# Gated projection of the state space layer: high parts written block by block, low parts consumed one by one, and the combined outputs turned at other places

## The chip, the cores and the metric

The kernel runs on one core of a Trainium2 chip. The metric is the device time of one execution in microseconds (us); a kernel's time is the median of its runs.

## What is computed

One inference step of a hybrid decoder with two layers, for a prompt of 1024 tokens and 8 x 8 sample tokens with the same weights. All 1088 tokens stand side by side as columns (with 4 columns of padding: `T` = 1092). The first layer has three dilated attention groups and a state space layer (S5) side by side; the change lies in the tail of that layer:

```python
out_a = (num / den[..., None]).reshape(n, t, D_A)          # three attention groups combined
y, h_last = s5_scan(u, ...)                                # (tokens, 512)
zb = jax.nn.gelu(y)
out_b = zb * jax.nn.sigmoid(zb @ w_glu + b_glu)            # the gated projection, 512 x 512
mix = jnp.concatenate([out_a, out_b], axis=-1) @ w_out_ab  # 1024 x 1024
```

The products are taken in float32 as three products of split operands: a value is a high part (rounded to `fp32r`) plus a low part (the rest), and high x high, high x low and low x high are summed in PSUM.

## The kernel before, in words

**How a product is tiled.** Weights come in slots of 1.1 MB. SP loads a slot into `w_raw` (`feed`, line 351), POOL splits it into `w_hi` and `w_lo` (lines 656 and 658), and TensorE (PE) uses it in `features` (line 770). Two split buffers alternate, so POOL splits slot n + 2 when PE has finished slot n (`slot_done`). One output unit of 128 features is three PSUM banks of 364 columns. For each of its k-chunks of 128 input features PE runs 9 matmuls, line 784: three operand pairs times three column blocks. The units alternate between PSUM banks 0 to 2 and 3 to 5; banks 6 and 7 are left for turning tiles. The gated projection (slot `W_GLU`) has 4 units of 4 k-chunks, so 36 matmuls per unit; a slot of the output projection (`W_OUT`) has 2 units of 8 k-chunks.

**The stage around the change, per engine.** Every engine has its own program in order, tied by semaphores.

- PE computes the scan's block outputs in two halves (`block_outputs`, lines 1060 and 1065) for z = 0 and z = 1, two blocks r each, and turns them back to feature rows (line 1095). Then it waits until all four low parts of `zb` are made (`lo_made`, line 1099), and runs `features` on `W_GLU`. After each unit m `mixed_pair(m)` (line 1103) turns two of the eight tiles of `out_a` in banks 6 and 7 (line 1112), the first time after the load of `mix_in`, and from the second pair on after DVE has read both banks (`mix_low`). Before `W_OUT` it waits for all low parts and for `mix_low` 8.
- ACT copies the block outputs (line 1458), applies Gelu to each of four blocks r of `zb` (line 1467) and, after all four, writes the four high parts `z_hi` (`high`, line 1261, from the loop at 1470). In the GLU loop it takes each unit with Sigmoid (`take`, line 1271), copies the two turned tiles into the high part `h_hi` of the output projection's input (line 1485), and makes the high part of a gated unit one unit later.
- DVE clears the padding of `zb` (line 2142), makes the four low parts `z_lo` (`low`, line 1670), then per unit multiplies the sigmoid with `zb` (line 2152), makes the low part of the gated unit (line 1670), and makes the two low parts of the turned tiles (line 2158).
- SP loads `mix_in` when the last block output is made (`y_mm` 4). When everything of the layer's combined output is made (`LO_MIXED_A` and `mix_low` 8) it loads the old residual `xd` (4.4 MB) and goes on feeding slots, the next being slot 23. Slots 21 and 22 (the first two of `W_OUT`) have been loaded by then, and slot 21 is split.
- POOL splits slot 22 when PE has finished `W_GLU`.

`z_hi`, then `z_lo` lie in the region `xa`, which held `d_mat` (front part) and `b_mat` (back part) of the scan until shortly before.

Of the kernel before, what the change touches and what calls it, by code (L numbers as in the profile page):

```python
# [20 lines left out]
P = 128  # L21
# [87 lines left out]
def build(nc, a):  # L109
# [16 lines left out]
    with ExitStack() as ctx:  # L126
# [14 lines left out]
        def sem(name):  # L141
# [32 lines left out]
            [("ca", 2 * ST * 9 * 16, F32), ("ub", L_BLK * 512, F32)],  # L174
            [("kc_sb", 2 * T, F32), ("vc_sb", 9 * 256, F32), ("qc_st", 2048, F32), ("on_c", 1024, F32)])
        hid_hi, hid_lo = (hid_hi0, hid_hi1), (hid_lo0, hid_lo1)
        (xa, z_hi, z_lo, sp_t, qb, qs, so, c_acc, bt, _, x12, _, bm_e, d_mat, _, b_mat,
         cs_s, cs_t, ocs, cstat) = region(
            "xa", KC * T,
            [("z_hi", 4 * T, F32R), ("z_lo", 4 * T, F32R)],  # L180
            [("sp_t", 12 * P, F32), ("qb", 768, F32), ("qs", 12 * SAMPLE, F32), ("so", 256, F32), ("c_acc", 1024, F32)],
            [("bt", 4096, F32), ("e3", 32, F32), ("x12", 2 * 2304, F32)],
            [("e4", 4128, F32), ("bm_e", 4096, F32)],
# [52 lines left out]
        def tiles(t, n):  # L236

            return t[:, :].rearrange("p (n c) -> p n c", n=n)
# [441 lines left out]
        def _(pe):  # L680
# [86 lines left out]
                            mean_square(2, True)  # L767
                rms.add(6)

            def features(slot, XH, XL, kcs=KC, n_units=2, done=1, arriving=False, after={}, kcs_used=False):  # L770

                WH, WL = halves(slot, kcs)
                for m in range(n_units):
                    cols = slice(m * P, m * P + P)
                    s = m % 2
                    late(free[s], u.free[s].at)
                    u.free[s].add()
                    for kc in range(kcs):
                        if arriving and m == 0:
                            pe.wait_ge(lo_made, lo.add())  # L780
                        for w, x in ((WH, XH), (WL, XH), (WH, XL)):
                            first, last = kc == 0 and w is WH and x is XH, kc == kcs - 1 and x is XL
                            for c in range(3):
                                mm = pe.matmul(UNIT[s][:, c, :], w[:, kc, cols], x[:, kc, c * CH:(c + 1) * CH],  # L784
                                               start=first, stop=last)
                        if kcs_used and m == n_units - 1 and kc < kcs - 1:
                            mm.then_inc(kc_used, 1)
                    if m == n_units - 1:
                        mm.then_inc(slot_done, done)
                        u.done.add(done)  # L790
                    else:
                        mm.then_inc(full, 1)
                        u.full.add()
                    if m in after:
                        after[m]()
# [300 lines left out]
                    mm.then_inc(turn_mm, 1)  # L1096


            pe.wait_ge(lo_made, lo.add(4))
            slot_ready()  # L1100


# [9 lines left out]
                        mm = pe.transpose(psum[:, 6 + b, c * P:c * P + P], mix_in[:, t * 512 + c * P:t * 512 + c * P + P], ident[:, :])  # L1112
                    mm.then_inc(turned, 1)

            features(W_GLU, ZH, ZL, kcs=4, n_units=4, after={k: lambda k=k: mixed_pair(k) for k in range(4)})
            lo.add(4)


            lo.add()
# [1 line left out]
            for layer in range(2):  # L1121
# [50 lines left out]
                pe.wait_ge(lo_made, lo.at)  # L1172
                for k in range(3):
                    slot_ready()
                    features(W_OUT[layer] + k, HH, HL)
                mixed_tail(W_OUT[layer] + 3)

                up = W_FF[layer]
# [44 lines left out]
        def _(act):  # L1223
# [230 lines left out]
            for z in range(2):  # L1454
                for r in (2 * z, 2 * z + 1):
                    act.wait_ge(y_mm, r + 1)
                    for h in range(2):
                        act.activation(groups(YT, r, h), psum[:, 2 * r + h, :].rearrange("p (k s c) -> p k s c", k=4, s=L_BLK),
                                       ACT.Copy).then_inc(y_taken, 1)
                if z == 0:  # L1460
                    act.wait_ge(turn_mm, 1)
                    act.activation(ZB[:, :, 0:SAMPLE], psum[:, 4, 0:4 * SAMPLE].rearrange("p (m t) -> p m t", m=4),
                                   ACT.Gelu_apprx_tanh).then_inc(act_own, 1)
                    own.add()
                for r in (2 * z, 2 * z + 1):
# [10 lines left out]
            lo.add()  # L1476
            for m in range(4):
                if m >= 2:
                    act.wait_ge(lo_made, lo.at + m - 1)
                take(TMP[:, m % 2, :], m, m == 3, ACT.Sigmoid, bias=param[:, C_GLU + m:C_GLU + m + 1])  # L1480
                if m:
                    high(HH[:, 3 + m, :], TMP[:, (m - 1) % 2, :], scaled, scl.add())
                for b in range(2):
                    act.wait_ge(turned, n_turn.add())
                    act.activation(HH[:, 0:4, SAMPLE + (2 * m + b) * P:SAMPLE + (2 * m + b + 1) * P],
                                   psum[:, 6 + b, :].rearrange("p (k c) -> p k c", c=P), ACT.Copy).then_inc(mix_high, 1)
            high(HH[:, 7, :], TMP[:, 1, :], scaled, scl.add())
            lo.add(4)


            for layer in range(2):
                if layer == 1:
# [12 lines left out]
                    act.wait_ge(zeroed, 4)  # L1505
                    attend(0, H_C)
                    lo.add(8)
                    for n in range(NB):
# [139 lines left out]
        def _(dve):  # L1648
# [489 lines left out]
            dve.tensor_tensor(STS[:, 0], HV[:, 0, :, N_BLK + 1:], SX[0], ALU.add)  # L2138
            dve.tensor_tensor(STS[:, 1], HV[:, 1, :, N_BLK + 1:], SX[2], ALU.add)
            dve.tensor_copy(st_o[:, 0:2 * ST].rearrange("p (c j) -> p c j", c=2), HV[:, :, :, N_BLK]).then_inc(state_out, 1)  # L2140
            dve.wait_ge(turn_mm, 1)
            dve.memset(ZB[:, :, PADS:T], 0.0).then_inc(zeroed, 1)
            for m in range(4):
                low(ZL[:, m, :], ZB[:, m, :], ZH[:, m, :])


            dve.memset(HH[:, 0:4, PADS:T].bitcast(F32), 0.0)
            dve.memset(HL[:, 0:4, PADS:T].bitcast(F32), 0.0)
            low(HL[:, 0:4, 0:SAMPLE], tiles(oas, 4), HH[:, 0:4, 0:SAMPLE])
            for m in range(4):  # L2150
                dve.wait_ge(free[m % 2], UNITS_AT[W_GLU] // 2 + m // 2 + 1)
                dve.tensor_tensor(TMP[:, m % 2, :], TMP[:, m % 2, :], ZB[:, m, :], ALU.mult).then_inc(scaled, 1)
                low(HL[:, 4 + m, :], TMP[:, m % 2, :], HH[:, 4 + m, :])
                for b in range(2):
                    t = 2 * m + b
                    cols = slice(SAMPLE + t * P, SAMPLE + t * P + P)
                    dve.wait_ge(mix_high, t + 1)
                    dve.tensor_tensor(HL[:, 0:4, cols], psum[:, 6 + b, :].rearrange("p (k c) -> p k c", c=P), HH[:, 0:4, cols].bitcast(F32),
                                      ALU.subtract).then_inc(mix_low, 1)
            u.skip(4)  # L2160


# [302 lines left out]
```

## Time and profile before

| what | value |
|---|---|
| runs | 3629.39, 3631.47 and 3649.05 us; median 3631.47 us |
| the profiled execution | 3641.45 us, of which the profile's span is 3639.6 us |
| busy share of the span | PE 91%, weight loads 87%, DVE 39%, ACT 25%, POOL 21% |
| granted TensorE clock, mean | 0.955 of full speed |

The span is what the profile shows from the first instruction to the last. The busy share of PE is an average over stages; the stage of the change lies from about 1020 to 1135 us. In the page's 40 slices of 91 us it is the one from 1001 to 1092 us (busy tenths of PE 8, granted clock 7 tenths) and the one behind it.

Three views are read below. The chain of waits follows the work that ended last back to what released it. The waits give, for each engine, the idle time and what ended it. The windows give busy time and granted clock of each engine in a stretch: a clock of 0.50 is 1.2 GHz and 1.00 is 2.4 GHz.

### The profile page before, as it was taken

To read this page: it belongs to the slowest core of one execution; us is meant where nothing else is said; L and a number is where in the kernel's file an instruction comes from. 1 tells how busy PE (TensorE), PEld (TensorE's weight loads), DVE (VectorE), ACT (ScalarE), POOL (GpSimd) and SP (SyncE) were. 2 spreads that over 40 slices of the span, in tenths; PEclk is the share of its full clock that TensorE was granted. 3 is DMA by queue.
4 is the path that set the end of the run, shared out by engine and by line. 5 is a ranking of instruction groups with operands and counts; after the bars stand their busy time and mean duration, and the time that the engine had idled before them with its cause. 6 is when DMAs were issued, how large, how long until landed. Compare 5 with 4: busy or idle time off the path is not lost.

```text
span 3639.6 us, 50510 instructions
## 1 busy us (share of the span) xinstructions
PE 3310.4 (91%) x21025; PEld 3163.5 (87%) x21025; DVE 1402.4 (39%) x1852; ACT 907.6 (25%) x1876; POOL 779.6 (21%) x226
## 2 busy tenths in 40 slices
PE   5998999984578899999999899886989999999988
PEld 4997988983468799999999799876879999999988
DVE  7615012033442633333334571364254333333364
ACT  3116044061131500000001521474151000000151
POOL 2220220210002222333223222200112332233321
PEclk9999999987789999999999999998899999999999
DMA  3311320348802222221225021100112112222411
GB/s 112 120 66 39 116 89 26 114 156 292 282 28 87 87 84 95 84 83 63 92 95 203 25 94 43 42 0 32 74 74 78 55 64 80 80 80 80 161 38 62
DMA packets 84290, 325.26 MB, mean 89 GB/s; under 512 B 19056, under 2 KB 32176, under 8 KB 66096
## 3 DMA queue, kind: packets, MB, share of 16 engines
q1 hardware_dynamic: 84160, 323.41, 25.2%
q8 instruction: 96, 1.57, 0.2%
q14 instruction: 34, 0.28, 0.0%
HBM read 274.21 MB, written 107.46 MB: 105 GB/s over the span
## 4 chain that ended last, share of the span: by engine, by line
PE 79%; DVE 9%; ACT 6%; issue 3%; DMA 2%; SPq 1%; ACTq 0%; DVEq 0%
PE psum L784 61%; PE psum L809 6%; PE psum L856 2%; PE psum L725 2%; PE psum L881 2%; ACT pr L1313 1%; PE psum L759 1%; DVE stat L1810 1%; ACT pt L1321 1%; DVE xa L1733 1%; DVE sm L1805 1%; DVE rs L1680 1%; DVE h_lo L1670 1%; DVE xa L1741 1%; PE psum L983 1%
## 5 line engine op out<-in xcount | busy, mean ns | idle before, releaser
L656 POOL CAST w_hi<-w_raw 128x2184 fp32r<-128x2184 f32 x109 | 222.8, 2044 | 2782.3 <-PE psum L784 2096.4
L784 PE MATMUL psum<-h_hi,w_hi 128*128 128x364 f32 x2832 | 627.6, 330 | 16.6 <-DVE tmp L2232 6.8
L784 PE MATMUL psum<-h_lo,w_hi 128*128 128x364 f32 x2544 | 563.6, 329 | 5.9 <-DVE h_hi L1710 5.9
L658 POOL TENSOR_TENSOR w_lo<-w_raw,w_hi 128x2184 fp32r<-128x2184 f32 x109 | 542.7, 4979 | 8.7
L784 PEld LDWEIGHTS psum<-h_hi,w_hi 128*128 128x128 f32 x2832 | 494.9, 189 | 18.0 <-DVE tmp L2232 7.4
L784 PE MATMUL psum<-h_hi,w_lo 128*128 128x364 f32 x2304 | 509.6, 329 | 0.0
L2248 DVE TENSOR_TENSOR xa<-xa,psum 128x1092 f32<-128x1092 f32 x256 | 330.8, 1292 | 382.6 <-PE psum L784 382.3
L784 PEld LDWEIGHTS psum<-h_lo,w_hi 128*128 128x128 f32 x2544 | 441.7, 189 | 6.4 <-DVE h_hi L1710 6.2
L784 PEld LDWEIGHTS psum<-h_hi,w_lo 128*128 128x128 f32 x2304 | 400.6, 189 | 0.0
L1592 ACT ACTIVATE tmp<-tmp 128x1092 f32<-128x1092 f32 x64 | 71.6, 1118 | 1255.6 <-DVE tmp L2232 1255.6
L784 PE MATMUL psum<-hid_hi,w_hi 128*128 128x364 f32 x1536 | 338.7, 328 | 5.2 <-DVE xa L2248 5.2
L784 PE MATMUL psum<-hid_lo,w_hi 128*128 128x364 f32 x1536 | 339.9, 330 | 0.0
L784 PE MATMUL psum<-hid_hi,w_lo 128*128 128x364 f32 x1536 | 339.2, 329 | 0.0
L1805 DVE TENSOR_TENSOR sm<-psum,mask 128x512 f32<-128x512 f32 (+1 forms) x160 | 94.5, 590 | 515.0 <-PE psum L856 511.1
L2232 DVE SCALAR_TENSOR_TENSOR tmp<-psum,sq 128x1092 f32<-128x1092 f32 x64 | 82.7, 1295 | 533.4 <-PE psum L784 508.8
L784 PEld LDWEIGHTS psum<-hid_hi,w_hi 128*128 128x128 f32 x1536 | 267.8, 189 | 5.8 <-DVE xa L2248 5.8
L784 PEld LDWEIGHTS psum<-hid_lo,w_hi 128*128 128x128 f32 x1536 | 267.1, 188 | 0.0
L784 PEld LDWEIGHTS psum<-hid_hi,w_lo 128*128 128x128 f32 x1536 | 266.7, 188 | 0.0
L809 PE MATMUL psum<-w_hi,h_hi 128*128 128x256 f32 x648 | 184.9, 285 | 21.8 <-DVE h_lo L1670 20.1
L809 PE MATMUL psum<-w_hi,h_lo 128*128 128x256 f32 x648 | 183.8, 284 | 0.0
L1313 ACT ACTIVATE pr<-sm,stat 128x256 f32<-128x256 f32 (+1 forms) x320 | 147.1, 460 | 90.4 <-DVE stat L1810 45.3
L809 PE MATMUL psum<-w_lo,h_hi 128*128 128x256 f32 x576 | 163.7, 284 | 0.0
(317 smaller groups left out, 4395.8 us busy)
## 6 DMA issues: line engine op xcount, KB each, us to landing
w_raw<-in_wall SPq DMA_DIRECT2D x111, 1092.0 KB, 5.0
kt_sb<-in_kt SPq DMA_DIRECT2D x16, 1024.0 KB, 11.3
out_ovs<-in_v SPq DMA_DIRECT2D x8, 2032.0 KB, 15.5
x_keep<-xa SPq DMA_DIRECT2D x2, 4368.0 KB, 11.8
xd_late<-x_keep SPq DMA_DIRECT2D x2, 4368.0 KB, 13.9
out_oks<-in_kt SPq DMA_DIRECT2D x8, 1008.0 KB, 7.9
out_ovs<-in_v SPq DMA_DIRECT2D x8, 1008.0 KB, 8.9
og<-o_st SPq DMA_DIRECT2D x24, 264.0 KB, 2.0
```

The source lines that it names most:

```text
L656: pool.tensor_copy(high[:, :], w_raw[:, :]).then_inc(hi_made, 1)
L658: pool.tensor_tensor(low[:, :], w_raw[:, :], high[:, :].bitcast(F32), ALU.subtract).then_inc(split, 1)
L725: mm = pe.matmul(UNIT[m][:, c, :], w[:, kc, m * P:m * P + P], x[:, kc, c * CH:(c + 1) * CH], start=kc == 0 and w is WH and x is XH, stop=k ...
L784: mm = pe.matmul(UNIT[s][:, c, :], w[:, kc, cols], x[:, kc, c * CH:(c + 1) * CH], start=first, stop=last)
L809: mm = pe.matmul(psum[:, 3 * s + c, 0:256], x[:, kc], w[:, kc, :], start=kc == 0 and x is XH and w is WH, stop=kc == KC - 1 and x is XL)
L856: mm = pe.matmul(psum[:, k % 2, hh * 256:hh * 256 + nk * P], staged[:, h, :], K[:, kt], start=True, stop=True)
L881: mm = pe.matmul(psum[:, 4 + h // 8, (h % 8) * HEAD_DIM:(h % 8 + 1) * HEAD_DIM], pt[:, o:o + P], vals[:, bass.ds(t, 1), c:c + HEAD_DIM], s ...
L1313: mm = act.activation(pr[:, o:o + nk * P], sm[:, o:o + nk * P], ACT.Exp, bias=stat[:, h:h + 1], accum_out=stat[:, 16 + h:17 + h])
L1592: act.activation(TMP[:, m, :], TMP[:, m, :], ACT.Square).then_inc(act_own, 1)
L1805: dve.tensor_tensor(out, psum[:, k % 2, :].rearrange("p (h c) -> p h c", h=2)[:, :, 0:nk * P], m.unsqueeze(1).broadcast_to([P, 2, nk * P]) ...
L2232: dve.scalar_tensor_tensor(chunked(TMP[:, m, :]), UNIT[m], 0.0, chunked(rs2), ALU.max, ALU.mult).then_inc(free[m], 1)
L2248: dve.tensor_tensor(chunked(XA[:, m, :]), chunked(XA[:, m, :]), UNIT[m % 2], ALU.add).then_inc(free[m % 2], 1)
```

## The change

1. `z_lo` and `z_hi` change places in the region `xa`: `z_lo` now lies where `d_mat` was, `z_hi` where `b_mat` was.
2. ACT clears the padding of `zb` itself (a copy of 16 columns with scale 0) and writes the high part of each block r right after that block's Gelu, for r = 0 and 1 before the block outputs of r = 2 and 3 are copied.
3. DVE waits for `y_mm` 4 and makes the four low parts as their high parts come.
4. PE no longer waits for all four low parts: the first unit of `W_GLU` waits before each k-chunk for the low part of that chunk.
5. `mixed_pair(1)` moves into the middle of unit 1 (between its k-chunks 1 and 2), pairs 2 and 3 come after units 1 and 2, and nothing is turned after unit 3. ACT's and DVE's programs follow that order, and ACT makes a gated unit's high part in the same turn instead of one unit later.
6. Before the first slot of `W_OUT` PE waits for the low part of the sample columns and `mix_low` 8 only; in that slot's first unit it waits before each of the k-chunks 4 to 7 for the low part of that chunk.

```diff
-        (xa, z_hi, z_lo, sp_t, qb, qs, so, c_acc, bt, _, x12, _, bm_e, d_mat, _, b_mat,
+        (xa, z_lo, z_hi, sp_t, qb, qs, so, c_acc, bt, _, x12, _, bm_e, d_mat, _, b_mat,
...
-            [("z_hi", 4 * T, F32R), ("z_lo", 4 * T, F32R)],
+            [("z_lo", 4 * T, F32R), ("z_hi", 4 * T, F32R)],
...
     # TensorE: features()
                     for kc in range(kcs):
-                        if arriving and m == 0:
+                        if kc == kcs // 2 and m in midway:
+                            midway[m]()
+                        if arriving and m == 0 and kc >= arriving_from:
                             pe.wait_ge(lo_made, lo.add())
...
-            pe.wait_ge(lo_made, lo.add(4))
             slot_ready()
...
-            features(W_GLU, ZH, ZL, kcs=4, n_units=4, after={k: lambda k=k: mixed_pair(k) for k in range(4)})
-            lo.add(4)
+            features(W_GLU, ZH, ZL, kcs=4, n_units=4, arriving=True, midway={1: lambda: mixed_pair(1)},
+                     after={0: lambda: mixed_pair(0), 1: lambda: mixed_pair(2), 2: lambda: mixed_pair(3)})
...
-                    features(W_OUT[layer] + k, HH, HL)
+                    features(W_OUT[layer] + k, HH, HL, arriving=layer == 0 and k == 0, arriving_from=4)
...
     # ScalarE
                 if z == 0:
                     act.wait_ge(turn_mm, 1)
+                    act.activation(ZB[:, :, PADS:T], ident[:, 0:16].rearrange("p (m t) -> p m t", m=4), ACT.Copy, scale=0.0)
...
                     own.add()
-            act.wait_ge(zeroed, 3)
-            for m in range(4):
-                high(ZH[:, m, :], ZB[:, m, :], act_own, own.at)
+                    high(ZH[:, r, :], ZB[:, r, :], act_own, own.at)
             lo.add(4)
...
                 take(TMP[:, m % 2, :], m, m == 3, ACT.Sigmoid, bias=param[:, C_GLU + m:C_GLU + m + 1])
-                if m:
-                    high(HH[:, 3 + m, :], TMP[:, (m - 1) % 2, :], scaled, scl.add())
-                for b in range(2):
-                    act.wait_ge(turned, n_turn.add())
-                    act.activation(HH[:, 0:4, ...], psum[:, 6 + b, :]..., ACT.Copy).then_inc(mix_high, 1)
-            high(HH[:, 7, :], TMP[:, 1, :], scaled, scl.add())
+                if m < 3:
+                    mixed_pair((0, 2, 3)[m])
+                high(HH[:, 4 + m, :], TMP[:, m % 2, :], scaled, scl.add())
+                if m == 0:
+                    mixed_pair(1)
...
     # VectorE
-            dve.wait_ge(turn_mm, 1)
-            dve.memset(ZB[:, :, PADS:T], 0.0).then_inc(zeroed, 1)
+            dve.wait_ge(y_mm, 4)
             for m in range(4):
                 low(ZL[:, m, :], ZB[:, m, :], ZH[:, m, :])
...
                 dve.tensor_tensor(TMP[:, m % 2, :], TMP[:, m % 2, :], ZB[:, m, :], ALU.mult).then_inc(scaled, 1)
+                if m < 3:
+                    mixed_pair((0, 2, 3)[m])
                 low(HL[:, 4 + m, :], TMP[:, m % 2, :], HH[:, 4 + m, :])
-                for b in range(2):
-                    ...
+                if m == 0:
+                    mixed_pair(1)
```

In ACT's and DVE's new `mixed_pair(k)` stand the same two copies and the same two subtractions as before; DVE also waits for `state_out`, its own earlier instruction. Nothing else changes: the numbers of matmuls, transposes, copies and subtractions are the same, save DVE's clearing of the padding, which ACT does.

## Rows read from the trace of the kernel before

**Rows 1.** Page, the chain that ended last, shares by line.

```profile
PE psum L784 61%; PE psum L809 6%; PE psum L856 2%; PE psum L725 2%; PE psum L881 2%; ACT pr L1313 1%; PE psum L759 1%; DVE stat L1810 1%; ACT pt L1321 1%; DVE xa L1733 1%; DVE sm L1805 1%; DVE rs L1680 1%; DVE h_lo L1670 1%; DVE xa L1741 1%; PE psum L983 1%
```

**Rows 2.** Chain of waits, 1036 to 1108: start us, us, what.

```profile
1044.18 4.92 DVE z_lo L1670 x4
...
1049.15 8.28 PE psum L784 x36
1057.43 0.87 PE psum L1112 x8
1058.31 6.01 PE psum L784 x36
...
1094.27 5.78 DVE h_lo L1670
...
1106.89 1.28 PE psum L784 x3
```

**Rows 3.** Waits, 1037 to 1135: engine, line, releaser: us in total, times, longest.

```profile
PE psum L1112 <- DVE h_lo L2158: 17.2, 3, 8.7
...
PE psum L784 <- DVE z_lo L1670: 8.8, 1, 8.8
...
PE psum L784 <- DVE h_lo L2158: 4.2, 1, 4.2
```

**Rows 4.** Windows: length, busy of PE, PEld, DVE, ACT, POOL, granted clock, DMA.

```profile
1038.00:1040.30 2.30, 2.14 (x18) 1.67 (x16) 0.00 (x0) 2.23 (x3) 0.00 (x0) 1.00 0.33 85
1049.10:1053.80 4.70, 4.65 (x16) 4.65 (x17) 0.37 (x3) 0.00 (x0) 0.00 (x0) 0.52 0.00 0
1068.40:1074.00 5.60, 5.50 (x21) 5.50 (x22) 1.84 (x3) 1.19 (x2) 0.00 (x0) 0.50 0.01 3
1082.40:1087.80 5.40, 5.38 (x20) 5.38 (x21) 1.77 (x2) 1.19 (x2) 0.00 (x0) 0.50 0.00 0
1100.70:1102.70 2.00, 1.97 (x8) 1.57 (x8) 1.75 (x2) 0.60 (x1) 0.00 (x0) 0.50 0.00 0
1106.80:1111.30 4.50, 4.41 (x14) 4.41 (x15) 1.01 (x2) 0.00 (x0) 0.00 (x0) 0.50 0.76 264
```

**Rows 5.** Timeline of PE: start us, us, engine, line, instruction [idle before].

```profile
1039.21 1.09 PE L1095 MATMUL psum<-ident,ub 128*128 128x128 f32 x8 [0.16 <-ACT ub L1458]
```

**Rows 6.** Groups by form, 1037 to 1107: busy us, mean ns | idle before.

```profile
L2152 DVE TENSOR_TENSOR tmp<-tmp,zb 128x1092 f32<-128x1092 f32 x4 | 5.1, 1286 | 9.2 <-ACT tmp L1271 9.2
L2158 DVE TENSOR_TENSOR h_lo<-psum,h_hi 128x512 fp32r<-128x512 f32 x8 | 5.1, 681 | 0.0
...
L1271 ACT ACTIVATE tmp<-psum,param 128x1092 f32<-128x1092 f32 x4 | 4.7, 1172 | 27.6 <-PE psum L784 27.6
L1485 ACT ACTIVATE h_hi<-psum 128x512 fp32r<-128x512 f32 x8 | 4.7, 597 | 14.7 <-PE psum L1112 14.7
...
L1261 ACT ACTIVATE z_hi<-zb 128x1092 fp32r<-128x1092 f32 x4 | 4.1, 1101 | 0.1
```

**Rows 7.** Timeline of ACT, 1024 to 1048.

```profile
1026.86 0.38 ACT L1462 ACTIVATE zb<-psum 128x256 f32<-128x256 f32 x1
...
1032.93 1.09 ACT L1458 ACTIVATE ub<-psum 128x512 f32<-128x512 f32 x2 [1.91 <-PE psum L1065]
...
1039.09 3.86 ACT L1467 ACTIVATE zb<-psum 128x1024 f32<-128x1024 f32 x2
```

**Rows 8.** DMA issues, 1000 to 1180: count, KB each, median us to landing.

```profile
xd<-in_xT SPq DMA_DIRECT2D x1, 4368.0 KB, 14.3
...
mix_in<-mix SPq DMA_DIRECT2D x1, 2048.0 KB, 8.2
```

**Rows 9.** Timeline of all engines, where POOL and DVE both read SBUF.

```profile
1094.12 4.78 POOL L658 TENSOR_TENSOR w_lo<-w_raw,w_hi 128x2184 fp32r<-128x2184 f32 x1
...
1232.46 2.70 POOL L656 CAST w_hi<-w_raw 128x2184 fp32r<-128x2184 f32 x1 [44.20 <-DVE h_lo L1710]
...
1233.22 2.34 DVE L1710 SCALAR_TENSOR_TENSOR h_lo<-xa,param,h_hi 128x364 fp32r<-128x364 f32 x1
```

More of the change, by code:

```diff
@@ L768, in arrive, with features @@
                 rms.add(6)
-            def features(slot, XH, XL, kcs=KC, n_units=2, done=1, arriving=False, after={}, kcs_used=False):
+            def features(slot, XH, XL, kcs=KC, n_units=2, done=1, arriving=False, arriving_from=0, after={}, midway={},
+                         kcs_used=False):
                 WH, WL = halves(slot, kcs)
@@ L1476, in _, with mixed_pair @@
             lo.add()
+            def mixed_pair(k):
+                for b in range(2):
+                    act.wait_ge(turned, n_turn.add())
+                    act.activation(HH[:, 0:4, SAMPLE + (2 * k + b) * P:SAMPLE + (2 * k + b + 1) * P],
+                                   psum[:, 6 + b, :].rearrange("p (k c) -> p k c", c=P), ACT.Copy).then_inc(mix_high, 1)
             for m in range(4):
@@ L1480, in _ @@
                 take(TMP[:, m % 2, :], m, m == 3, ACT.Sigmoid, bias=param[:, C_GLU + m:C_GLU + m + 1])
-                if m:
-                    high(HH[:, 3 + m, :], TMP[:, (m - 1) % 2, :], scaled, scl.add())
-                for b in range(2):
-                    act.wait_ge(turned, n_turn.add())
-                    act.activation(HH[:, 0:4, SAMPLE + (2 * m + b) * P:SAMPLE + (2 * m + b + 1) * P],
-                                   psum[:, 6 + b, :].rearrange("p (k c) -> p k c", c=P), ACT.Copy).then_inc(mix_high, 1)
-            high(HH[:, 7, :], TMP[:, 1, :], scaled, scl.add())
+                if m < 3:
[3 more added lines that the diff above has]
+                    mixed_pair(1)
             lo.add(4)
@@ L1504, in _ @@
                     u.all_free(act)
-                    act.wait_ge(zeroed, 4)
+                    act.wait_ge(zeroed, 3)
                     attend(0, H_C)
@@ L2140, in _ @@
             dve.tensor_copy(st_o[:, 0:2 * ST].rearrange("p (c j) -> p c j", c=2), HV[:, :, :, N_BLK]).then_inc(state_out, 1)
-            dve.wait_ge(turn_mm, 1)
-            dve.memset(ZB[:, :, PADS:T], 0.0).then_inc(zeroed, 1)
+            dve.wait_ge(y_mm, 4)
             for m in range(4):
                 low(ZL[:, m, :], ZB[:, m, :], ZH[:, m, :])
+            dve.wait_ge(state_out, 1)
             dve.memset(HH[:, 0:4, PADS:T].bitcast(F32), 0.0)
@@ L2149, in _, with mixed_pair @@
             low(HL[:, 0:4, 0:SAMPLE], tiles(oas, 4), HH[:, 0:4, 0:SAMPLE])
+            def mixed_pair(k):
+                for t in (2 * k, 2 * k + 1):
+                    cols = slice(SAMPLE + t * P, SAMPLE + t * P + P)
+                    dve.wait_ge(mix_high, t + 1)
+                    dve.tensor_tensor(HL[:, 0:4, cols], psum[:, 6 + t % 2, :].rearrange("p (k c) -> p k c", c=P),
+                                      HH[:, 0:4, cols].bitcast(F32), ALU.subtract).then_inc(mix_low, 1)
             for m in range(4):
@@ L2152, in _ @@
                 dve.tensor_tensor(TMP[:, m % 2, :], TMP[:, m % 2, :], ZB[:, m, :], ALU.mult).then_inc(scaled, 1)
+                if m < 3:
+                    mixed_pair((0, 2, 3)[m])
                 low(HL[:, 4 + m, :], TMP[:, m % 2, :], HH[:, 4 + m, :])
-                for b in range(2):
[L2155 to L2159, printed above, removed]
+                if m == 0:
+                    mixed_pair(1)
             u.skip(4)
```

## Prediction

> **What bounds the kernel now.** I read the page first: the chain that ended last is mostly one PE line, the split-operand matmuls [rows 1], so the kernel is bound by PE where PE is fed, and a stage is worth what PE loses in it. Then I read the chain of waits and the waits of PE in the stage of the change. PE's last turn of scan outputs ends at 1039.21 + 1.09 = 1040.30 [rows 5], and its first matmul of the output projection starts at 1106.89 [rows 2]: 66.6 us. In them PE stands idle 8.8 us until the last of four low parts of `zb`, three times at a pair of tiles until DVE has read the banks of the pair before (17.2 us in all, the longest 8.7), and 4.2 us until the last low parts before `W_OUT` [rows 3]: 30.2 us. The longest wait has a reason of its own: one low part took DVE 5.78 us, where four of the same size took 4.92 together, while POOL was splitting slot 22 [rows 2, 9]. Last I read the granted clock in windows: after each idle time PE ran at half clock for a while. What that costs is length times (1 - clock): 4.7 x 0.48 = 2.3, 5.6 x 0.5 = 2.8, 5.4 x 0.5 = 2.7, 2.0 x 0.5 = 1.0, and 4.5 x 0.5 = 2.2 behind the stage, at the start of `W_OUT` [rows 4]. So 30.2 us idle and 8.8 us of slow clock lie in the stage, 2.2 us behind it: 41.2 us. The rest is work: a unit of 36 matmuls takes 6.01 us (1.50 per k-chunk), a pair of tiles 0.87 us [rows 2]; 4 x 6.01 + 4 x 0.87 = 27.5 us, and 66.6 - 39.0 = 27.6.
>
> **The change, part by part.** None of this work goes away. The question is how much waiting is left, so I lay out the new order, with about 0.05 us for each handing over.
>
> *High parts block by block.* ACT writes the high parts of r = 0 and 1 (1.10 us each [rows 6]) behind their Gelus. Queued behind them is the copy of block outputs r = 2, before which ACT sat idle 1.91 us [rows 7]. It moves by 2.2 - 1.91 = 0.3 us, with the padding's copy by up to 0.7. What waits for it on PE is the turn of r = 2, which stands behind all of r = 3's block outputs; ACT's copies of those come 5 us after the copy of r = 2 [rows 7]. So nothing on the path. The padding's copy lies between that of DVE's memset it replaces and the sample Gelu's 0.38 us [rows 7]; PE's second half of blocks waits for that Gelu, but for DVE's scan too. I take 0 and keep 0.4 for the range.
>
> *Low parts one by one.* DVE now waits for the last block output (about 1038.0: the Gelu of r = 2 starts at 1039.09, behind the 1.09 us of ACT's copies of r = 3 [rows 7]). Queued behind that wait are only the low parts and the sample columns, and DVE had nothing to do there before. Low 0 and 1 (1.29 us each, as DVE's product of the same size [rows 6]) are ready by 1040.7. PE starts k-chunk 0 at 1040.3 in place of 1049.15, k-chunk 1 at 1041.8, done 1043.3. Gelu r = 2 from 1039.09 takes about 2.0 (two in 3.86), its high part 1.10, its low part 1.29: 1043.65, so PE waits 0.35. The next block follows on ACT: Gelu until 1044.2, high 1045.35, low 1046.7. PE finished k-chunk 2 at 1045.15 and waits 1.55. Unit 0 ends at 1048.2.
>
> *The pairs.* `mix_in` is issued by the same event as before and landed 8.2 us later [rows 8], at 1046.3; pair 0 wants it at 1048.2, so its cover shrinks from 11 to 1.9 us; beyond that each us late is one of PE. Pair 0 ends at 1049.1, half of unit 1 at 1052.1. There pair 1 sits between two matmuls of one unit: whatever it waits for stops the rest of unit 1. It needs DVE's reading of pair 0: Sigmoid 1.17 from 1048.25, DVE's product 1.29, two reads of 0.6 to 0.7 [rows 6]: 1052.0. ACT's two copies (0.60 each) run beside the product. That is no wait, but with 0.1 us to spare; I allow 0.5. From there the cover grows: pair 2 wants at 1056.0 what DVE has done by 1054.5, pair 3 at 1062.9 what is done by 1060. Unit 1 ends at 1056.0, unit 2 at 1062.9, unit 3 at 1069.7. ACT's and DVE's new orders keep up: per unit each has some 4 us in 6.9.
>
> *The start of `W_OUT`.* After unit 3 nothing is turned. `mix_low` 8 is there by 1067 (Sigmoid of unit 2 at 1062.95, product, two reads). So PE goes on at 1069.7 in place of 1106.89. Its k-chunk 7 wants the last low part at 1069.7 + 7 x 1.50 = 1080.2. That comes from Sigmoid until 1070.9, then DVE's product; but POOL starts splitting slot 22 at 1069.75. DVE's two-input work stands still beside POOL's cast, as at 1233.22 (2.34 us in place of 0.59), and beside its subtraction, as at 1094 [rows 2, 9]. I let the product run between the two, until 1073.0; the high part 1074.1; the subtraction, 4.8 us, until 1077.8; the last low part 1.15 later, as in the trace: 1079.0. Cover 1.2 us. If the product loses to both, it is 1080.5, a wait of 0.3. The 5.78 us of before are still there, but under k-chunks 0 to 6.
>
> *SP and POOL.* The load of `xd` and the feed of slot 23 now start some 9 us after `W_OUT` begins, not with it. `xd` took 14.3 us and slot 23 has a quarter of its bytes: some 18 us, until 1097; slot 21 ends at 1069.7 + 24.0 = 1093.7, the split takes 7, so 1104 against 1117.8, when PE wants slot 23. `xd` is needed only after the four slots. Hidden. Slot 22 is split 16 us before its turn. Swapping `z_lo` and `z_hi` costs nothing: same instructions.
>
> **Sum.** Of 41.2 us, 1.9 (0.35 + 1.55) come back as new waits: a gain of 39.3 us. The stage goes from 66.6 to 29.4 us, and 2.2 us of slow clock behind it go. The profiled execution, 3641.45 us, would be 3602.2. It lies 10.0 us above the median shown, 3631.47; the gain doesn't depend on that, so the median goes to **3592.2 us**.
>
> **A rule against it.** The turns up to 1040.3 ran at a granted clock of 1.00 [rows 4], and my sum lets PE go on at full clock through the waits of 0.35 and 1.55 us; whether stretches so mixed hold it, no row shows. The Trainium skill, in "TensorE: Matmul & The Clock Gate", section on the PE-mode transpose, says that a transpose doesn't count as PE being busy the way a matmul does. By that the clock could fall in unit 0, since turns lie before it and two waits in it. The row shows the turns at full clock, not what comes of them. By the row the time is 3592.2, by the rule that of the first rival.
>
> **Rivals.**
> - *The clock falls in unit 0.* For it: turns before, waits inside. Against: the turns that followed other matmuls were at 1.00 [rows 4]. Price: unit 0 took 8.28 in place of 6.01 us after a long idle time [rows 2]. Gain 37.0, 3594.5 us. Chance 0.09; this is what the rule just named would do.
> - *The change doesn't do what it says:* the low parts still come as one burst, because DVE or ACT holds the first back. Then PE starts at 1046.7 with a cold unit (8.28), and 4 x 0.87 + 3 x 6.01 follow: `W_OUT` at 1076.5, gain 30.4 + 2.2 = 32.6, 3598.9 us. Against: nothing in ACT's or DVE's order stands between. Chance 0.04.
> - *The pairs' wait comes back.* Pair 1 stops unit 1 for what DVE hasn't read, and pairs 2 and 3 in turn: three waits of 4.2 us, as the short ones of now, and after each 2.7 us of slow clock [rows 3, 4]: 20.7 back, gain 18.6, 3612.9 us. For it: 0.1 us of cover at pair 1. Against: one late pair doesn't make the next late, the cover grows. Chance 0.04.
> - *Slower: the clock isn't given back.* If stops and turns keep PE at half clock from unit 0 on, a matmul takes 4.41 / 14 = 0.315 us [rows 4] in place of 0.167. The gain is used up after 39.3 / 0.148 = 266 matmuls, from `W_GLU`'s 144 into `W_OUT`'s first slot. If it lasts to the end of slot 22 (432), 64 us are lost: 25 us slower, 3656 us. Against: after each stop of now the clock was back within 6 us [rows 4]. Chance 0.02.
>
> **How the numbers follow.** The forecast has 0.81. Low end: all 41.2 us, and 4.6 us more should one clash of POOL and DVE of the kind of [rows 9] shift off the path elsewhere: 3631.5 - 45.8 = 3585.7. High end: the pairs' rival, 3612.9, which is also the forecast with the spread of the runs shown above their median (17.6 us) and some of the 0.4, 0.5 and 0.3 us. Rounded, 3586 to 3613. A difference of 0.5% (18.2 us) is about what a measurement of this kernel can tell from no change; the forecast is 1.08%. "Same" gets half of the pairs' rival and 0.02 for a disturbed measurement, "slower" its 0.02: 0.94, 0.04, 0.02.
>
> **What the changed profile would show.** PE's first `W_GLU` matmul right behind the turns near 1040, two short waits on `z_lo` inside unit 0, no wait on DVE's reads (line 2158) at the pairs, `W_OUT` starting some 29 us after the last turn, a granted clock near 1.00 from there to the end of `W_OUT`, one stretched DVE low part beside POOL's split with no PE wait after it, and no POOL wait on the load of slot 23 that reaches PE. Wrong would be: a PE wait over 2 us at a pair or at k-chunk 7, `mix_in` landing after unit 0, half clock after unit 0, or a gap on PE before slot 23.

## The result and the profile after

| | before | changed |
|---|---|---|
| median of 6 runs each | 3635.15 us (3629.39 to 3649.05) | 3605.01 us (3598.36 to 3606.23) |
| ratio | | 0.9902, 95% interval 0.9882 to 0.9922 |
| the profiled execution, its span | 3641.45, 3639.6 us | 3605.07, 3603.3 us |
| busy: PE, weight loads, DVE, ACT, POOL | 91, 87, 39, 25, 21% | 92, 88, 39, 25, 22% |
| granted clock, mean | 0.955 | 0.957 |

The changed kernel is faster by 1% (1 - 0.9902, times 3635.15: 35.6 us, from 28 to 43; the two medians lie 30.1 us apart). The forecast was a gain of 39.3 us and a median of 3592.2; the gain lies in the interval, the median came out 12.8 us above and inside the range. Of the 12.8, 3.7 are the median of before, which six runs put at 3635.15 and not at 3631.47; the rest is what the medians' 30.1 us lack of 39.3.

The page's chain still ends in the split-operand matmuls, which are line 787 now, with the share of [rows 1]:

```profile
PE psum L787 61%; PE psum L812 6%; PE psum L725 2%; PE psum L859 2%; PE psum L884 2%; ACT pr L1315 1%; PE psum L759 1%; DVE stat L1815 1%; ACT pt L1323 1%; DVE xa L1738 1%; DVE sm L1810 1%; DVE rs L1685 1%; ACT q_st L1300 1%; DVE xa L1746 1%; PE psum L986 1%
```

The chain of waits of the changed kernel, 1036 to 1110 (start us, us, what), answers to [rows 2]:

```profile
1044.10 1.12 ACT z_hi L1263
1045.22 2.09 ACT zb L1470
1047.33 1.12 ACT z_hi L1263
...
1048.48 1.31 DVE z_lo L1675
...
1049.83 1.76 PE psum L787 x9
1051.59 0.87 PE psum L1114 x8
1052.46 3.03 PE psum L787 x18
1055.49 0.87 PE psum L1114 x8
1056.37 2.98 PE psum L787 x18
1059.35 0.87 PE psum L1114 x8
1060.22 6.00 PE psum L787 x36
1066.22 0.87 PE psum L1114 x8
1067.10 42.93 PE psum L787 x258
```

Read it from the bottom. From 1049.83 on every piece is PE's and each begins where the one before it ended: four pairs of 0.87 us between matmuls, and then unit 3 and `W_OUT` as one piece, which ends at 1110 only because the view does. Above that the chain is ACT's, high part and Gelu in turn, with one low part at its end, where [rows 2] had a burst of four. The waits of PE in the changed kernel, 1015 to 1112 (us in total, times, longest), answer to [rows 3]:

```profile
PE psum L1063 <- DVE hv L2129: 2.9, 1, 2.9
PE psum L787 <- DVE z_lo L1675: 1.9, 2, 1.5
PE psum L1098 <- ACT ub L1460: 0.2, 1, 0.2
```

Of the 30.2 us that PE stood idle in the stage 1.9 are left: the two waits on low parts inside unit 0, 0.43 and 1.47 us. Nothing waits on line 2158's successor at the pairs, and nothing before `W_OUT`. But a row stands on top that [rows 3] doesn't have: 2.9 us until DVE's scan, ahead of the stage. The windows of the changed kernel (columns as in [rows 4]) show what follows that wait, and the clock in the stage:

```profile
1027.90:1033.70 5.80, 5.80 (x30) 4.68 (x30) 1.96 (x9) 3.83 (x3) 0.00 (x0) 0.50 0.09 25
1033.70:1040.80 7.10, 7.10 (x70) 5.77 (x69) 0.00 (x0) 1.08 (x2) 0.00 (x0) 0.99 0.01 2
1043.10:1046.10 3.00, 3.00 (x19) 2.76 (x17) 1.17 (x2) 2.97 (x3) 0.00 (x0) 1.00 0.95 358
1046.10:1051.40 5.30, 3.40 (x19) 3.03 (x19) 2.11 (x5) 3.90 (x4) 0.00 (x0) 1.00 0.43 161
1073.00:1086.00 13.00, 13.00 (x80) 13.00 (x79) 7.62 (x3) 3.13 (x3) 7.84 (x2) 1.00 0.25 85
```

In the stage the clock is at 1.00 (2.4 GHz) from the first k-chunk on, through both waits, and at the start of `W_OUT` PE gets 80 matmuls done in 13 us. The half clock lies earlier: the second half of the block outputs began at 0.50 (1.2 GHz) and took 12.90 us; before it took 10.30.

So the two spans, 36.3 us apart, divide like this. `z1` is the start of the block outputs' second half, "blocks" its length up to the first turn, "stage" runs from the end of the last turn to the first matmul of `W_OUT`, "rest" from there to the end of the span:

| profile | wait before z1 | z1 | blocks | last turn ends | `W_OUT` | stage | rest |
|---|---|---|---|---|---|---|---|
| before | 0.97 | 1027.66 | 10.30 | 1040.30 | 1106.89 | 66.59 | 2532.7 |
| changed | 2.93 | 1027.90 | 12.90 | 1043.14 | 1072.92 | 29.78 | 2530.4 |

The stage gives 36.8 us and the rest 2.3, and 2.84 are lost ahead of the stage: 0.24 at z1, 2.60 in the blocks. In the rest, `W_OUT` gives 2.25 by itself: from its first matmul to PE's next idle time, 1.26 us that both kernels have, it took 74.33 us before (1106.89 to 1181.22) and 72.08 now (1072.92 to 1145.00). That all of the rest differs by no more than that is chance, since it will be seen to vary by 10 us from profile to profile of the same code.

### The profile page after: what moved, and what is told of

Its sections match the earlier page's. It is cut to its first block, busy times and chain, and to the rows that moved or that the text cites. A ratio compares the mean times of both kernels' runs of the same rounds, so it can differ in the third digit from the quotient of the medians.

```text
span 3603.3 us, 50510 instructions
## 1 busy us (share of the span) xinstructions
PE 3303.3 (92%) x21025; PEld 3160.1 (88%) x21025; DVE 1396.5 (39%) x1851; ACT 908.5 (25%) x1877; POOL 782.4 (22%) x226
## 4 chain that ended last, share of the span: by engine, by line
PE 79%; DVE 9%; ACT 6%; issue 3%; DMA 2%; SPq 1%; ACTq 0%; DVEq 0%
PE psum L787 61%; PE psum L812 6%; PE psum L725 2%; PE psum L859 2%; PE psum L884 2%; ACT pr L1315 1%; PE psum L759 1%; DVE stat L1815 1%; ACT pt L1323 1%; DVE xa L1738 1%; DVE sm L1810 1%; DVE rs L1685 1%; ACT q_st L1300 1%; DVE xa L1746 1%; PE psum L986 1%
```

## The experiments

Three questions: do the parts of the change pay what my terms say, was the half clock a cost of its own in the kernel before, and does the half clock in the block outputs come from the change? The rival to my theory in the first four runs was that one part makes the whole gain and the rest is cover.

**e1_lows_only: parts 1 to 4 alone.**

```diff
+            features(W_GLU, ZH, ZL, kcs=4, n_units=4, arriving=True, after={k: lambda k=k: mixed_pair(k) for k in range(4)})
             lo.add(4)
```

(with the diff's lines of ACT, of DVE and of the region `xa`; the pairs and the wait before `W_OUT` stay as before)

> Parts 1 to 4 of the change alone (high parts block by block, low parts one by one); the pairs, the orders of the GLU loop and the start of W_OUT stay as before. Theory (the gain is the sum of the waits removed, each where it stands): the first unit of W_GLU ends about 9.2 us earlier after the last turn (8.8 us idle and 2.3 us of slow clock go, 1.9 us of waits between k-chunks come); the three waits at the pairs (17.2 us) and the 4.2 us before W_OUT stay as they are. Last turn to W_OUT 66.6 - 9.2 = 57.4 us, kernel 9 us faster than before (0.25%). Rival (the low parts come as one burst still): 64 us, 2.5 us faster. Rival (the time is set by the chain of ACT and DVE that ends before W_OUT): about 66 us, no gain.

**e2_pairs_only: part 5 alone**, the diff's lines on `midway` and `mixed_pair`, with all four low parts still waited for at once.

```diff
+            features(W_GLU, ZH, ZL, kcs=4, n_units=4, midway={1: lambda: mixed_pair(1)},
+                     after={0: lambda: mixed_pair(0), 1: lambda: mixed_pair(2), 2: lambda: mixed_pair(3)})
             lo.add(4)
```

> Part 5 alone (pair 1 in the middle of unit 1, pairs 2 and 3 after units 1 and 2, a gated unit's high part in the same turn); low parts of zb in one burst and the full wait before W_OUT as before. Theory: the three waits at the pairs (17.2 us) and the slow clock after them (6.5 us) go; unit 3 ends 21.5 us after unit 0, and the wait before W_OUT grows from 4.2 to 9.3 us, since all of the last gated unit's chain (Sigmoid, product, high part, low part beside POOL's split) now stands there. Last turn to W_OUT 66.6 - 18.7 = 47.9 us, kernel 18.7 us faster (0.5%). Rival (pair 1 stops unit 1 and the waits come back at the new places): 60 us or more. Rival (POOL's clash with DVE was most of the wait at pair 3, and stays on the path): the same 47.9 us, since it is in the 9.3 us.

**e3_wout_only: part 6 alone.**

```diff
-            lo.add(4)
...
-                    features(W_OUT[layer] + k, HH, HL)
+                    features(W_OUT[layer] + k, HH, HL, arriving=layer == 0 and k == 0, arriving_from=4)
```

> Part 6 alone (W_OUT waits chunk by chunk for the last four low parts); everything before it stays. Theory: no gain by itself, because pair 3 is still read after the last low part, so mix_low 8 lets W_OUT start at the same time: last turn to W_OUT 66.6 us, kernel within 1 us of before. Rival (the wait before W_OUT is for the low parts, and each part of the change gives its own share): 4.2 us idle and some of the slow clock go, 62 us, kernel 4 to 6 us faster.

**e4_no_wout: the changed kernel without part 6** (the same lines the other way round).

> The whole change but part 6: W_OUT waits for all low parts again. Theory: unit 3 ends as in the changed kernel, 29.7 us after the last turn, then PE waits 9.3 us for the last low part (made beside POOL's split) and runs W_OUT's first 4.5 us at half clock (2.2 us): last turn to W_OUT 39 us; kernel 11.5 us slower than the changed one, 25 to 28 us faster than before. Rival (the last low part is no longer late once a gated unit's high part is made in the same turn): 31 us, within 2 us of the changed kernel.

Measured on one chip beside before's 3641.65 us (22 runs):

| kernel | median us | ratio, 95% | gain of it, us | stage us | gain in the stage |
|---|---|---|---|---|---|
| parts 1 to 4 | 3627.63 | 0.9973, 0.996 to 0.9986 | 9.8 | 56.63 | 9.96 |
| part 5 | 3616.75 | 0.9946, 0.9921 to 0.9971 | 19.7 | 48.28 | 18.31 |
| part 6 | 3640.06 | 1.0002, 0.9988 to 1.0017 | -0.7 | 66.52 | 0.07 |
| 1 to 5 | 3617.51 | 0.9938, 0.9918 to 0.9959 | 22.6 | 39.05 | 27.54 |

In the stage all four came near what was expected of them (57.4, 47.9, 66.6 and 39 us). The waits of PE from 1015 to behind the stage say which idle time each part takes away. Parts 1 to 4:

```profile
PE psum L1114 <- DVE h_lo L2159: 17.2, 3, 8.7
PE psum L787 <- DVE h_lo L2159: 4.2, 1, 4.2
PE psum L787 <- DVE z_lo L1671: 1.9, 2, 1.4
```

Part 5:

```profile
PE psum L787 <- issue: 9.1, 1, 9.1
PE psum L787 <- DVE z_lo L1678: 8.8, 1, 8.8
PE psum L1063 <- DVE hv L2132: 2.8, 1, 2.8
```

Part 6:

```profile
PE psum L1115 <- DVE h_lo L2160: 17.2, 3, 8.7
PE psum L787 <- DVE z_lo L1672: 8.8, 1, 8.8
PE psum L787 <- DVE h_lo L2160: 4.2, 1, 4.2
```

Parts 1 to 4 turn the 8.8 us at `z_lo` into 1.9 and leave the waits at the pairs as they were. Of their 9.96 us, 1.26 lie behind the first two of these waits all the same: pair and unit took 8.78 and 9.21 us there, not 9.69 and 9.56, because the half clock ended sooner in this profile (0.70 over the 5.6 us behind the first wait, where [rows 4] has 0.50). That much a gain in the stage can owe to the clock of one profile. Part 5 takes all of the 17.2 and 4.2 us and leaves the 8.8. But it puts up a wait of its own: 9.1 us before `W_OUT`, to which the profile gives no releaser ("issue"). In this kernel PE stands there at the wait for all low parts; the timeline of part 5's DVE shows what it stands there for, the last low part stretched to 4.62 us under POOL's split:

```profile
1082.56 4.62 DVE L1678 TENSOR_TENSOR h_lo<-tmp,h_hi 128x1092 fp32r<-128x1092 f32 x1 [1.18 <-ACT h_hi L1265]
```

It ended at 1087.18, and PE's first matmul of `W_OUT` followed at 1087.29. Part 6 alone leaves all three waits in place, since PE still waits for `mix_low` 8 there. So the parts don't add up one by one: 1 to 4 and 5 do (9.96 + 18.31 = 28.27, together 27.54), and part 6 is worth 0.07 us alone and 39.05 - 29.78 = 9.27 on top of parts 1 to 5. The rival of one part that makes the gain falls: two have one of their own, and the third gets its worth from the wait that part 5 uncovers.

**e10_pair1_early: pair 1 one k-chunk earlier in unit 1**, to measure the cover of the one pair that I had with 0.1 us to spare (a single run).

```diff
-                        if kc == kcs // 2 and m in midway:
+                        if kc == 1 and m in midway:
```

> The changed kernel with pair 1 one k-chunk earlier (between k-chunks 0 and 1 of unit 1). Theory (pair 1 is placed with almost no cover: DVE has read pair 0 about when k-chunk 1 ends): PE now stops inside unit 1 for 1.0 to 1.5 us until DVE's reads, and the last turn to W_OUT takes 30.6 to 31.1 us in place of 29.6. Rival (DVE has read pair 0 long before): no wait, 29.6 us.

The timeline of its PE at pair 1:

```profile
1048.27 0.66 PE L787 MATMUL psum<-z_lo,w_hi 128*128 128x364 f32 x3
1049.75 1.25 PE L1114 MATMUL psum<-ident,mix_in 128*128 128x128 f32 x8 [0.82 <-DVE h_lo L2159]
```

PE waits 0.82 us, and the eight turns take 1.25 us where they take 0.87 behind running matmuls: 1.20 us, and the stage grew by as much, 29.78 to 30.94. Pair 0 began at 1046.39, so DVE had read its banks 3.36 us after it began; in the changed kernel pair 1 comes 0.87 + 3.03 = 3.90 us after pair 0. The cover there is 0.5 us, not 0.1. PE waits tile by tile (`mix_low` t - 1): the first tile of a pair needs only the first of DVE's two reads, and not both, as the text on the kernel before and my sum have it. DVE's two reads ran from 1049.01 to 1050.29 in this profile, and PE went on at 1049.75, behind the first.

**e5_filled_waits: the kernel before, with matmuls without use in its idle times**, to take away the half clock and leave the waits (they write PSUM banks that are free there and are cleared by the next product).

```diff
+            def filler(n, bank):
+                w = w_hi[buffer_of(W_OUT[0])]
+                for _ in range(n):
+                    pe.matmul(psum[:, bank, 0:CH], w[:, 0:P], w[:, 0:CH], start=True, stop=True)
...
+            filler(44, 0)
             pe.wait_ge(lo_made, lo.add(4))
...
+                else:
+                    pe.wait_ge(free[(k + 1) % 2], u.free[(k + 1) % 2].at)
+                    filler(44 if k == 3 else 17, 3 * ((k + 1) % 2))
...
+            filler(17, 0)
             pe.wait_ge(mix_low, 8)
```

> The kernel before, with nothing of the change, but with extra matmuls on PE in its five idle stretches between the last turn and W_OUT (44, 17, 17, 44 and 17 matmuls of 364 columns, about 7.3 and 2.8 us each at full clock; their results are written over). This measures by itself what the slow clock costs. Theory (11.0 us of the 41.2 are PE at half clock after idle time): the waits stay and end at the same events, but PE starts at full clock behind each, so the last turn to W_OUT takes 66.6 - 8.8 = about 58 us and W_OUT's start gains 2.2 us more; kernel 9 to 11 us faster than before. Rival (PE's slow starts are something else than the clock, or the chain of ACT and DVE sets the end): 66 us or longer, kernel not faster.

3638.21 us beside 3642.01, ratio 0.9982 (0.9966 to 0.9999): 6.6 us, from 0.4 to 12, so by the time alone only just faster; the stage took 60.0 in place of 66.6. Its windows (columns as in [rows 4]): block outputs, unit 0, start of `W_OUT`:

```profile
1028.00:1046.40 18.40, 18.40 (x96) 14.87 (x96) 1.98 (x10) 1.69 (x3) 0.00 (x0) 0.50 0.03 9
1058.60:1064.90 6.30, 6.27 (x38) 6.24 (x39) 0.35 (x3) 0.00 (x0) 0.00 (x0) 1.00 0.01 3
1109.00:1113.50 4.50, 4.42 (x26) 4.42 (x27) 0.99 (x2) 0.00 (x0) 0.00 (x0) 1.00 0.86 311
```

With PE kept at work unit 0 ran at 1.00 and took 6.26 us, not 8.28, and `W_OUT` got 26 matmuls done in its first 4.5 us, not 14 as in [rows 4]. So the half clock was a cost, and matmuls in the waits give it back. The size is short of what I had expected, by 2.2 us in the stage. Three differences come to about that: unit 0 takes 6.26 where running matmuls need 6.01 (0.25), the three pairs behind a wait 1.25 where 0.87 (1.14), and `z_lo` came 9.5 us after the last turn, not 8.8 (0.7), in a profile whose block outputs ran at half clock for the whole of their second half; that this is the reason isn't shown. The first two are what PE needs to get going again behind a wait at full clock; I had put all of it down to the clock. That sum is worked out from rows, it wasn't tried by itself.

**e6_after_again and e11_after_third: the changed kernel twice more**, with no edit, and **e7_warm_gap: nine such matmuls ahead of the wait for the scan**:

```diff
+                if z:
+                    pe.wait_ge(split, W_OUT[0] + 1)
+                    w = w_hi[buffer_of(W_OUT[0])]
+                    for _ in range(9):
+                        pe.matmul(psum[:, 7, 0:CH], w[:, 0:P], w[:, 0:CH], start=True, stop=True)
                 pe.wait_ge(hp_made, z + 1)
```

> The changed kernel once more. The first profile of it lost 2.9 us of the forecast gain before the stage: PE waited 2.9 us for DVE's scan and ran the next blocks at half clock, where the kernel before waited 1.0 us and kept the clock. Theory (that is one of two states that both kernels have, set by whether the clock fell earlier, near 994 us, and has nothing to do with the change): either state may show here; in the state with the short wait the span is about 2.5 us shorter than in the other. Rival (the change brings the long wait): the long wait again, here and in every kernel with part 5 or the whole change, never in the kernel before. Ratio to the kernel before 0.989 to 0.992 in either case.

> The changed kernel with 9 extra matmuls of 364 columns on PE (1.5 us, results written over) in front of its wait for the second half of DVE's scan. Theory: PE idles at most 1.5 us there, the clock stays, and the second half of the block outputs takes 10.4 us, not 12.9, in whichever state the execution is: 0 to 2.5 us faster than the changed kernel, and at half a microsecond no slower where the wait was short. Rival (the slow blocks come from operands or PSUM, not from the clock): 12.9 us again.

> The changed kernel once more, on the same chip as the run with the filled gaps, as the one to compare that with. Theory: ratio to the kernel before 0.989 to 0.992, and the second half of the block outputs in one of its states (10.4, 12.9 or 18.5 us).

**e8_no_waits: e7, and k-chunks 0 and 1 of unit 1 put between k-chunks 1 and 2 of unit 0**, so that PE has work while the third and fourth low part are made; the pairs 1 and 2 follow later, after unit 1 and in the middle of unit 2.

```diff
+            for kc in range(2):
+                pe.wait_ge(lo_made, lo.add())
+                chunk(0, kc)
...
+            chunk(1, 0)
+            chunk(1, 1)
+            for kc in range(2, 4):
+                pe.wait_ge(lo_made, lo.add())
+                mm = chunk(0, kc)
+            unit_done(mm, 0)
+            mixed_pair(0)
+            chunk(1, 2)
+            unit_done(chunk(1, 3), 1)
+            mixed_pair(1)
...
```

> The changed kernel with the filler of the run before, and with k-chunks 0 and 1 of unit 1 taken between k-chunks 1 and 2 of unit 0 (pair 1 then stands behind unit 1, pair 2 in the middle of unit 2). Theory: both waits of unit 0 (1.9 us) are filled with work that is ready, so the last turn to W_OUT takes 27.6 us where the changed kernel takes 29.6; with the filler 2 to 4.5 us faster than the changed kernel (0.06 to 0.12%). Rival (pair 1 now stops PE, since unit 1 ends only 3.9 us after unit 0): a wait of 1 us or more at pair 1 takes half of it back, 28.6 us or longer.

**e9_no_waits_warm: e8 with 18 matmuls ahead of the wait for the scan**, not 9, and 9 more some 35 us earlier, ahead of the wait for the load of `d_mat`.

```diff
+            pe.wait_ge(v_taken, 8)
+            pe.wait_ge(split, W_OUT[0] + 1)
+            w = w_hi[buffer_of(W_OUT[0])]
+            for _ in range(9):
+                pe.matmul(psum[:, 4, 0:CH], w[:, 0:P], w[:, 0:CH], start=True, stop=True)
             pe.wait_ge(d_in, 16)
```

> The kernel of the run before (no waits in unit 0), with 18 instead of 9 extra matmuls (3.0 us) in front of PE's wait for the second half of the scan, and 9 more (1.5 us) where PE stood idle 1.8 to 3.1 us near 994, before the block outputs of the samples. Theory (the block outputs' time is set by whether the granted clock falls in those two idle stretches: 10.4 us at full clock, 12.9 or 18.5 us where it fell): PE idles less than 1.5 us in both, the clock stays, second half 10.4 us; last turn to W_OUT 27.6 us as before; 1 to 10 us faster than the run before by what that one lost, 0.3 to 0.4% faster than the changed kernel. Rival (in the second half the clock falls for a reason other than idle time): 12.9 or 18.5 us again.

| kernel | wait before z1 | z1 | blocks | stage | rest | median us | before there | ratio, 95% |
|---|---|---|---|---|---|---|---|---|
| e6, changed | 2.76 | 1027.85 | 10.29 | 29.77 | 2539.1 | 3610.06 | 3642.01 | 0.9903, 0.9884 to 0.9922 |
| e11, changed | 0.78 | 1021.59 | 10.27 | 29.80 | 2528.5 | 3601.69 | 3636.48 | 0.9901, 0.9882 to 0.992 |
| e7, filled wait | 1.44 | 1028.42 | 10.29 | 29.80 | 2530.7 | 3602.04 | 3642.01 | 0.9886, 0.9868 to 0.9904 |
| e8, no waits | 2.22 | 1027.34 | 18.45 | 27.29 | 2528.8 | 3598.27 | 3642.01 | 0.9876, 0.9858 to 0.9893 |
| e9, no waits | 0.16 | 1032.11 | 10.29 | 27.36 | 2528.6 | 3599.72 | 3636.48 | 0.9889, 0.9869 to 0.9909 |

The same kernel, profiled again in e6, kept the clock through a wait of 2.7 us (its windows before z1 and in the blocks):

```profile
1025.10:1027.80 2.70, 0.00 (x0) 0.00 (x0) 2.66 (x3) 2.66 (x4) 0.00 (x0) 1.00 0.00 0
1027.80:1038.20 10.40, 10.35 (x97) 8.42 (x98) 1.98 (x9) 5.11 (x5) 0.00 (x0) 1.00 0.05 16
```

So the 2.6 us that the changed kernel's first profile lost there are not a price of the change: the same code ran the blocks in 12.90, 10.29 and 10.27 us. Part 5 alone, which changes nothing ahead of the stage, had 12.88.

The long wait before z1 isn't the change's either. It goes with a stretch some 34 us earlier, where PE stands idle before the block outputs of the samples. Windows of before and of the changed kernel there:

```profile
994.00:1000.00 6.00, 5.85 (x49) 2.72 (x50) 5.93 (x17) 0.00 (x0) 0.00 (x0) 0.72 0.01 3
```

```profile
992.00:998.00 6.00, 4.09 (x48) 2.28 (x48) 5.90 (x12) 0.00 (x0) 0.00 (x0) 1.00 0.03 9
```

In five profiles (before, parts 1 to 4, part 6, e10, e11) PE had stood idle there for 3.10 to 3.50 us, the clock fell (0.72 in the 6 us behind it), the matmuls from there to the first turns took 30.4 to 30.5 us, and the wait before z1 was 0.78 to 0.97 us. In the other eight PE had been idle for 0.72 to 2.79 us, the clock stayed at 1.00, the same stretch took 28.95, and PE, there 1.5 us sooner, waited 2.76 to 3.74 us for the scan where no matmuls filled the wait. Both groups hold kernels with and without the change: e10 and e11 are in the first, e5, which has none of it, in the second. So the rival on record for e6 falls, and its theory, that both kernels do now the one and now the other, stands. The profile of before had lost its 1.5 us ahead of the wait for the scan, which became shorter by them; the changed kernel's first profile lost 2.6 us behind that wait. What sets the idle time near 994 isn't shown.

The nine matmuls of e7 left a wait of 1.44 us, and the clock held, as expected; the same nine left 2.22 us in e8, and it didn't.

In e8 and e9 PE waits for no low part and at no pair, and the stage shrinks by 2.4 to 2.5 us: the 1.9 us of waits and 0.5 that the two k-chunks behind them lose (1.76 us each in the chain of the changed kernel, 1.50 where matmuls run on). Windows of e9, blocks and stage, where the clock stayed at 1.00 throughout:

```profile
1032.10:1042.40 10.30, 10.29 (x96) 8.36 (x97) 1.97 (x9) 4.96 (x5) 0.00 (x0) 1.00 0.06 16
1044.70:1072.00 27.30, 27.30 (x177) 27.20 (x176) 15.96 (x20) 17.74 (x20) 0.00 (x0) 1.00 0.19 72
```

That the kernel's time falls too isn't shown: the ratios of e6 to e9 and e11 overlap, e9's expected gain over the changed kernel did not appear, and z1 alone lies between 1021.6 and 1032.1 us in these five profiles and the rest between 2528.5 and 2539.1. Two microseconds drown in that.

## Why the prediction held, and where its terms were off

- **What bounded the kernel** held: 30.2 us of idle time and the half clock behind it. Where the sum applies, it came out: 39.3 us forecast, 36.8 in the stage and 2.25 in `W_OUT` measured, 39.1. The experiments give the two groups of waits their own prices, 9.96 us for the low parts (idle 8.8 - 1.9; the rest clock, 1.26 of it not theirs) and 18.3 to 27.6 for the pairs and the start of `W_OUT`.
- **Low parts one by one.** They came singly and not in the burst of the second rival. Waits of 0.35 and 1.55 us were forecast; 0.43 and 1.47 were there. Left out was that a k-chunk behind a wait takes 1.76 us, not 1.50: 0.5 us for the two. Unit 3, which runs straight on into `W_OUT`, gave 0.2 back (5.82, not 6.01), and the stage was 29.8 us, not 29.4.
- **The pairs.** `mix_in` was issued at 1040.91 and landed 8.3 us later, at 1049.2; pair 0 wanted it at 1051.59. The cover forecast, 1.9 us, was 2.4, because unit 0 was longer. The cover at pair 1 was sized 0.1, with two of DVE's reads where PE waits for one, and is 0.5 (e10), so the pairs' rival had less for it than I gave it: even the pair that is late in e10 cost 1.2 us and no half clock.
- **The start of `W_OUT`** came as laid out: the last low part was forecast 9.3 us behind `W_OUT`'s first matmul, and came 1077.50 + 4.73 - 1072.92 = 9.31. PE wanted it at 1083.40, 1.2 us later, the cover forecast. The timeline of the changed kernel shows the race between POOL and DVE:

```profile
1073.16 2.01 POOL L656 CAST w_hi<-w_raw 128x2184 fp32r<-128x2184 f32 x1 [318.07 <-PE psum L787]
...
1074.39 1.92 DVE L2164 TENSOR_TENSOR tmp<-tmp,zb 128x1092 f32<-128x1092 f32 x1 [3.09 <-ACT tmp L1273]
...
1075.25 5.83 POOL L658 TENSOR_TENSOR w_lo<-w_raw,w_hi 128x2184 fp32r<-128x2184 f32 x1
...
1077.50 4.73 DVE L1675 TENSOR_TENSOR h_lo<-tmp,h_hi 128x1092 fp32r<-128x1092 f32 x1 [1.19 <-ACT h_hi L1263]
```

DVE's product, ready during the cast, ended 1.06 us after POOL's subtraction had begun, and the subtraction took 5.83 us where [rows 9] has 4.78: 1.05 more. The low part, ready during the subtraction, ended 1.15 us after it (1081.08), no longer than one alone takes (1.29). Each waited until the other's instruction was over. The Trainium skill says so in "SBUF — State Buffer", section "Terms": VectorE and GpSimd take the port pair they share by a lock that is held for a whole instruction, and the loser stands still. The trace agrees, with the 1.05 and 1.15 us. DVE's product, started at 1074.39, went ahead of POOL's subtraction, started at 1075.25.

- **SP and POOL** stayed hidden: slot 23 was issued at 1083.00, its cast began at 1098.19 and its subtraction ended at 1106.11, some 15 us before PE took the slot (1120.86); the next idle time of PE in the trace is the 1.26 us behind `W_OUT` (1145.00) that before has too.
- **High parts and padding at nothing** holds for the first profile. In e11, where z1 came 6 us earlier, PE was released by ACT's sample Gelu, not by the scan (`PE psum L1063 <- ACT zb L1465`, 0.8 us), and the copy of the padding, 0.22 us, lies in ACT's work ahead of it. At most that much is on the path there; 0.4 was kept.
- **The clock.** The rule that turns don't count as work would have cost 2.3 us in unit 0, the first rival. It did not: windows 1043.10 to 1051.40 are at 1.00, behind turns and through both waits, and in e5 and e8 the clock even rose during turns (last section). The dearest rival, a clock that isn't given back, did not come in the stage either. The step that failed ahead of the stage is one that I had not written down: **that everything up to 1040.30 takes as long as before.** The blocks' second half, just ahead of the stage, lost 2.60 us to the clock in the first profile, and nothing in the two later ones of the same code. What is left of the 12.8 us isn't traced to a place; it is inside the spread of this kernel's runs, 3598.36 to 3606.23 here and 3594.28 to 3603.39 in e11.

## What to carry to other kernels

Price an idle time of TensorE with what follows it, here 0.25 to 0.4 us for getting going again at full clock, and up to 2.8 us where the clock has fallen [rows 4]. Look for the waits in layers: moving the pairs was worth 9 us more once the wait that it uncovered was loosened too, and loosening that wait alone was worth nothing. When a gain of a few microseconds is to be shown, read it from the stage in the trace, since the time of a kernel whose clock varies elsewhere will not show it.

## What was not expected of the hardware

The second half of the block outputs, 32 matmuls and 64 smaller ones with PE never idle, took one of three times in thirteen profiles: 10.3 us at 1.00, 12.9 with the first 5.8 us at 0.50, or 18.45 at 0.50 to the end. Where the wait ahead of it was 0.16 to 1.44 us, in seven profiles, the clock held. The six longer waits aren't sorted by their length: after 2.76 us the clock held (e6), after 2.85 and 2.91 to 2.93 it was at half for 5.8 us (part 5 alone; 1 to 5 and the changed kernel), after 2.22 (e8, behind nine matmuls without use) and 3.74 us (e5) it stayed at half for the whole stretch. Windows of e8, the blocks and then a stretch of the 16 turns behind them, which begin at 1045.79:

```profile
1027.30:1045.80 18.50, 18.46 (x97) 14.88 (x97) 1.98 (x9) 4.27 (x5) 0.00 (x0) 0.50 0.03 9
...
1047.00:1047.50 0.50, 0.50 (x4) 0.50 (x3) 0.50 (x2) 0.00 (x0) 0.00 (x0) 0.50 1.04 102
1047.50:1048.00 0.50, 0.50 (x6) 0.50 (x5) 0.50 (x1) 0.22 (x1) 0.00 (x0) 0.90 0.54 188
```

PE was busy for 18.46 of 18.50 us, and the clock did not rise; it rose at about 1047.5, in the turns, before the first matmul of the gated projection (1048.37). In e5 it rose in the turns too: 0.50 until 1047.4, 1.00 from 1048.2, with the next matmuls of 364 columns from 1048.84 on. The Trainium skill, in "TensorE: Matmul & The Clock Gate", "Part 1: The HAM clock gate", says that the gate counts on its own time, whatever the program does, and that activity lifts it. With the first the trace agrees, as far as equal code and nearly equal waits ended differently; with the second these 18.46 us do not. What decides it here is open.
